# Top-1 and top-2 routing moved into the attention loop, tile by tile, in a hybrid decoder layer

## What is computed

```python
h2 = rms_norm(x2, ln2_g)
g_logits = h2 @ gw + gb                       # 4 expert groups
g_idx = argmax(g_logits); g_p = softmax(g_logits)[g_idx]
e_logits = (h2 @ ew + eb).reshape(T, 4, 8)[g_idx]
top_v, top_i = top_k(e_logits, 2)             # 2 of the group's 8 experts
gate = g_p * softmax(top_v); expert = g_idx * 8 + top_i
out = x2 + sum_r gate[r] * swiglu(h2, expert[r]);   final rms_norm
```

## Time and profile before

| | us |
|---|---|
| median of 3 runs | 1270.96 (1270.56 to 1271.1) |
| the profiled execution, its own time | 1266.62 |
| its span, first to last instruction | 1264.1 |
| TensorE busy in the span | 1139.6 |
| VectorE busy | 490.6 |
| ScalarE busy | 360.0 |
| GpSimd busy | 263.1 |

### The profile page before, as it was taken

The page is one execution under the profiler, slowest core; times in us unless marked ns, Lnnn a source line. Parts: engine busy times, 40 slices in busy tenths (PEclk is TensorE's granted clock), DMA queues, the critical chain, the costliest instruction groups (busy, mean ns, idle before and its releaser), DMA issues.

```text
span 1264.1 us, 16164 instructions
## 1 busy us (share of the span) xinstructions
PE 1139.6 (90%) x5013; PEld 548.1 (43%) x5014; DVE 490.6 (39%) x1018; ACT 360.0 (28%) x731; POOL 263.1 (21%) x226
## 2 busy tenths in 40 slices
PE   5999999998899999983699999989999999999930
PEld 4898444454356666643233333323333333333310
DVE  4360029942455666327323323322322332332217
ACT  3121100015465555310122232212322223222212
POOL 2010199920000000010211111121111111111113
PEclk9999999999799999995899999999999999999975
DMA  7317111012411111185590899999699998989036
GB/s 246 27 32 140 35 34 34 0 67 72 167 49 53 51 51 51 51 340 208 193 407 33 349 375 377 419 420 420 265 379 419 394 419 356 419 349 414 30 135 276
DMA packets 96315, 270.33 MB, mean 214 GB/s; under 512 B 42156, under 2 KB 59228, under 8 KB 71676
## 3 DMA queue, kind: packets, MB, share of 16 engines
q1 hardware_dynamic: 71060, 251.82, 52.0%
q0 software_dynamic: 8320, 16.80, 3.6%
q10 hardware_dynamic: 16872, 0.92, 0.9%
HBM read 253.25 MB, written 26.74 MB: 221 GB/s over the span
## 4 chain that ended last, share of the span: by engine, by line
PE 81%; DMA 7%; DVE 5%; ACT 2%; SPq 1%; issue 1%; ACTq 1%; POOLq 0%; POOL 0%; DVEq 0%
PE psum L1288 25%; PE psum L1021 13%; PE psum L1307 12%; PE psum L1203 9%; PE psum L1018 3%; PE psum L1161 3%; DMA W<-in_w_down 3%; PE psum L1181 2%; PE psum L1016 2%; PE psum L1276 2%; DMA W<-in_w_gate 2%; PE psum L1172 2%; PE psum L1295 2%; DMA W<-in_x 1%; PE psum L1226 1%
## 5 line engine op out<-in xcount | busy, mean ns | idle before, releaser
L1288 PE MATMUL psum<-W,RD 128*64 x800 | 366.8, 602 | 10.3 <-DVE RD L1775 10.3
L1289 PE MATMUL psum<-W,RD 128*64 128x512 f32 x800 | 366.8, 602 | 0.0
L1288 PEld LDWEIGHTS psum<-W,RD 128*64 128x64 f32 x800 | 106.2, 138 | 220.2 <-issue 214.3
L1307 PE MATMUL psum<-W,RD 128*64 x400 | 183.8, 602 | 3.2 <-ACT RD L944 2.4
L1308 PE MATMUL psum<-RD 128*64 128x512 f32 x400 | 183.8, 602 | 0.0
L1756 DVE TENSOR_TENSOR RD<-psum,RD 128x256 f32<-128x256 f32 x50 | 21.2, 424 | 414.2 <-ACT RD L940 414.2
L1021 PE MATMUL psum<-W 128*128 128x512 f32 x384 | 166.4, 593 | 0.6 <-ACT W L774 0.6
L699 POOL DMA_INDIRECT y_rows<-RD,tabi x49 | 51.9, 1059 | 472.8 <-ACT RD L951 453.5
L1203 PE MATMUL psum<-W,RD 128*128 128x512 f32 x256 | 120.0, 603 | 5.2 <-DVE W L1575 4.1
L1021 PEld LDWEIGHTS psum<-W 128*128 128x128 f32 x384 | 72.5, 190 | 89.7 <-issue 88.7
L1289 PEld LDWEIGHTS psum<-W,RD 128*64 128x64 f32 x800 | 106.2, 138 | 0.0
(11 more groups left out here) (315 smaller groups left out, 1290.7 us busy)
## 6 DMA issues: line engine op xcount, KB each, us to landing
W<-in_w_up SPq DMA_DIRECT2D x32, 2048.0 KB, 12.6
W<-in_w_gate SPq DMA_DIRECT2D x32, 2048.0 KB, 17.4
W<-in_w_down SPq DMA_DIRECT2D x32, 2048.0 KB, 19.2
W<-in_x SPq DMA_DIRECT2D x16, 512.0 KB, 5.0
W<-y_rows SPq DMA_DIRECT2D x16, 512.0 KB, 9.2
W<-in_w_in SPq DMA_DIRECT2D x5, 1024.0 KB, 12.6
W<-in_w_in SPq DMA_DIRECT2D x16, 256.0 KB, 4.3
x_rows<-W SPq DMA_DIRECT2D x8, 512.0 KB, 2.9
```

The costliest lines, as they stand in the source:

```text
L1288: pe.matmul(bank(2)[0:HALF].rearrange("p (g n) -> p g n", g=2), x, near, start=k == 0, stop=k == KD - 1)
L1289: ins = pe.matmul(bank(2)[HALF:P], x, upgate1[:, k].rearrange("p g n -> p (g n)"), start=k == 0, stop=k == KD - 1)
L1307: pe.matmul(out[0:HALF], a, W[:, bass.ds(base + (2 * KD * FF + D * k), 512)], start=k == 0, stop=k == FK - 1)
```

## The change

- The logits are made of x2 itself, not of h2: TensorE transposes x2 (`x2_turn`, half 0 at k = 4 i + 11, half 1 at k = 4 i + 13), multiplies at k = 4 i + 14, and VectorE multiplies with `rstd2` and adds the bias in one instruction. The loop has 44 iterations. h2 is still made and stored.
- VectorE picks the group (`pick_group`, k = 4 i + 14) and the experts (`pick_experts`, k = 4 i + 15) per tile. TensorE ranks tile i at k = 4 i + 18, ahead of the next tile's logits, with two bf16 matmuls (`rank`; `macc` is the sum of the tiles before). VectorE takes block and slot within the expert (`my_rank`, k = 4 i + 18) and writes `SI`, one-hot in the slot times the token's number.
- Behind the loop: the last tile's rank, the counts, the block numbers, 16 matmuls of 68 columns for the tokens, and the index table (`ids_ok`), on which the gathers start. The gates come after: VectorE turns `SI` into one-hot times gate (2048 elements), and TensorE does 16 more matmuls (`gate_ps`), ahead of the first turn of gathered rows. The table of blocks and experts has a block per partition and is turned into a row by 4 small matmuls. The first step's slot and counts are constants.
- `x2` has two buffers, not three; `xa` moves to where slot 0's gate goes, so that gate is loaded after the loop's last store; slot 2's down is loaded once the gates' matmuls have read `SI`.

```diff
-ITERS = 4 * (NT - 1) + 18
+ITERS = 4 * (NT - 1) + 16
@@ sync
-            load_gate(0)
             for i in range(NT):
 ...
+            load_gate(0)
             load_up(2)
             load_gate(2)
+            sp.wait_ge(gate_ps, 1)
             load_down(2)
@@ gpsimd
-            pool.wait_ge(idx_ok, 1)
+            pool.wait_ge(ids_ok, 1)
             for b in range(AHEAD):
                 gather(b)
+            pool.wait_ge(idx_ok, 1)
@@ tensor
+            def rank(i, out):
+                pe.wait_ge(mm_ok, i + 1)
+                ins = pe.matmul(out, tri[:, :], mbf[:, i, :], start=True, stop=i == 0)
+                if i:
+                    ins = pe.matmul(out, onesb[:, :], macc[:, i, :], start=False, stop=True)
+                return ins
 ...
-                    i = tile_at(k, 14 + b)
+                    i = tile_at(k, 11 + 2 * b)
                     if i is not None:
-                        h2_turn(i, b)
-                i = tile_at(k, 17)
+                        x2_turn(i, b)
+                i = tile_at(k, 14)
                 if i is not None:
+                    pe.wait_ge(h2T_ok, i + 1)
+                    if i:
+                        rank(i - 1, bank(5)[:, 64:96]).then_inc(rank_ps, 1)
                     logits(i)
 ...
+            rank(NT - 1, bank(0)[:, 0:32]).then_inc(rank_ps, 1)
+            pe.matmul(bank(1)[:, 0:32], onesb[:, :], macc[:, NT - 1, :], start=True, stop=False)
+            pe.matmul(bank(1)[:, 0:32], onesb[:, :], mbf[:, NT - 1, :], start=False, stop=True).then_inc(rank_ps, 1)
             for r in range(16):
                 if r % 8 == 0:
-                    pe.wait_ge(tab_ok, r // 8 + 1)
-                ins = pe.matmul(bank(2)[:, 0:2 * NBLK], slot1h[:, r, :], bval[:, r].rearrange("p n v -> p (n v)"),
-                                start=r == 0, stop=r == 15)
+                    pe.wait_ge(blk_ok, r // 8 + 1)
+                ins = pe.matmul(bank(2)[:, 0:NBLK], SI[:, r, :], blk1h[:, r, :], start=r == 0, stop=r == 15)
             ins.then_inc(tab_ps, 1)
 ...
+            pe.wait_ge(sg_ok, 1)
+            for r in range(16):
+                ins = pe.matmul(bank(3)[:, 0:NBLK], SI[:, r, :], blk1h[:, r, :], start=r == 0, stop=r == 15)
+            ins.then_inc(gate_ps, 1)
@@ vector
+            def pick_group(i):
+                dve.wait_ge(lg_ps, i + 1)
+                lg = logit[:, i, :]
+                dve.scalar_tensor_tensor(lg[:, 0:36], bank(5)[:, 0:36], rstd2[:, i:i + 1], rbias[:, :], ALU.mult, ALU.add).then_inc(lg_ok, 1)
+                dve.wait_ge(lg_ok, i + 1)
+                link(dve.max(mx8, lg[:, 32:40]))
+                dve.tensor_scalar(gdif[:, i, :], lg[:, 32:36], mx8[:, 0:1], None, ALU.subtract)
+                link(dve.max_index(gi8, mx8, lg[:, 32:40]))
+                link(dve.tensor_copy(gix[:, i:i + 1], gi8[:, 0:1]))
+                link(dve.tensor_scalar(goh, iotaf[:, 0:EGROUPS], gix[:, i:i + 1], None, ALU.is_equal))
+                link(dve.tensor_tensor(es4, ...))
+                link(dve.tensor_reduce(e8, es4.rearrange("p g n -> p n g"), AX.X, ALU.add))
+            def pick_experts(i):
+                link(dve.max(me8, e8))
+                dve.tensor_tensor(edif[:, i:i + 1], me8[:, 1:2], me8[:, 0:1], ALU.subtract)
+                link(dve.max_index(ei8, me8, e8))
+                dve.tensor_tensor(macc[:, i, :], macc[:, i - 1, :], mbf[:, i - 1, :], ALU.add)
+                link(dve.tensor_copy(idx2, ei8[:, 0:2]))
+                link(dve.scalar_tensor_tensor(idx2, idx2, float(EGROUPS), ...))
+                link(dve.tensor_tensor(MM[:, i], ..., ALU.is_equal))
+                dve.tensor_tensor(mbf[:, i, :], MM[:, i, 0, :], MM[:, i, 1, :], ALU.add).then_inc(mm_ok, 1)
+            def my_rank(i, src):
+                dve.wait_ge(rank_ps, i + 1)
+                dve.tensor_tensor(MP, MM[:, i], ..., ALU.mult).then_inc(rank_ok, 1)
+                dve.wait_ge(rank_ok, i + 1)
+                link(dve.tensor_reduce(rsel, MP, AX.X, ALU.add))
+                link(dve.tensor_scalar(lblk[:, i, :], rsel, ...))
+                link(dve.tensor_scalar(lblk[:, i, :], lblk[:, i, :], ROUND, ROUND, ALU.add, ALU.subtract))
+                link(dve.scalar_tensor_tensor(slot2, lblk[:, i, :], -float(HALF), rsel, ALU.mult, ALU.add))
+                for r in range(2):
+                    ins = dve.tensor_scalar(SI[:, 2 * i + r, :]..., slot2[:, r:r + 1], tokv[:, i, r:r + 1], ALU.is_equal, ALU.mult)
+                link(ins)
 ...
                 for b in range(2):
-                    i = tile_at(k, 14 + b)
+                    i = tile_at(k, 11 + 2 * b)
                     if i is not None:
-                        h2_turned(i, b)
+                        x2_turned(i, b)
+                i = tile_at(k, 14)
+                if i is not None:
+                    pick_group(i)
+                i = tile_at(k, 15)
+                if i is not None:
+                    pick_experts(i)
+                i = tile_at(k, 18)
+                if i is not None:
+                    my_rank(i, bank(5)[:, 64:96])
```

More of the change, by code:

```diff
@@ L254, in build, with late @@
+        d0 = 5120
+        def late(n):
+            nonlocal d0
+            d0 += n
+            assert d0 <= 5376
+            return RD[:, d0 - n:d0]
+        nb, bend, bs, ones, nn, below = late(32), late(32), late(32), late(32), late(6), late(32)
+        col = late(10)
+        stp = late(16)
+        gsum, den, gate = late(8), late(8), late(16).rearrange("p (t r) -> p t r", t=NT)
+        both = RD[:, 5700:5700 + 2 * NBLK].rearrange("p (n b) -> p n b", n=2)
         ident = sb("ident", [P, P])
@@ L425, in build @@
         ex_ye = sem("ex_ye")
-        x2_out = [sem(f"x2_out{i}") for i in range(3)]
+        x2_out = [sem(f"x2_out{i}") for i in range(2)]
         tail_y = sem("tail_y")
@@ L965, in step @@
                 actT_evac(b1)
+            step(0, 0)
             act.wait_ge(idx_ok, 1)
-            for b in range(4):
+            act.wait_ge(tabg_ok, 1)
+            for b in range(1, 4):
                 step(b // 2, b % 2)
@@ L1269, in _ @@
             ins.then_inc(tab_ps, 1)
+            pe.wait_ge(col_ok, 1)
+            for n_ in range(1 + SLOTS):
+                ins = pe.matmul(bank(7)[0:1, MAXBLK * n_:MAXBLK * (n_ + 1)], col[0:MAXBLK, n_:n_ + 1], ident[0:MAXBLK, 0:MAXBLK],
+                                start=True, stop=True)
+            ins.then_inc(col_ps, 1)
+            pe.wait_ge(sg_ok, 1)
+            for r in range(16):
+                ins = pe.matmul(bank(3)[:, 0:NBLK], SI[:, r, :], blk1h[:, r, :], start=r == 0, stop=r == 15)
@@ L1331, in step @@
                     down(bank(4 + (1 - q % 2)), prev, b, None if isinstance(freed, int) and freed <= 0 else freed)
+            xT(0, 16)
+            step(0, 0)
             pe.wait_ge(idx_ok, 1)
-            xT(0, 16)
-            for b in range(4):
+            for b in range(1, 4):
                 step(0, b)
@@ L1585, in _ @@
+            for k in range(ITERS):
+                if k == 6:
+                    dve.memset(logit, -3e38)
+                    dve.wait_ge(const_ok, 4)
+                    for r in range(2):
+                        ins = dve.tensor_scalar(tokv[:, :, r], tokf[:, :], 2.0, 2.0 * L * r - 4.0 * L, ALU.mult, ALU.add)
+                    link(ins)
                 for half in range(2):
@@ L1676, in _ @@
-            link(dve.reciprocal(gate[:, 0, :], den))
-            link(dve.tensor_tensor(gate[:, 1, :], gate[:, 0, :], eexp, ALU.mult))
-            dve.wait_ge(rank_ps, 1)
-            dve.tensor_copy(RK[:, :, :].rearrange("p t n -> p (t n)"), bank(0)[:, 0:256])
-            cnt, nb, bend, bs, ones = (ovt[:, 32 * q:32 * q + 32] for q in range(5))
+                    pick_group(i)
[3 more added lines that the diff above has]
+                i = tile_at(k, 18)
@@ L1712, in _ @@
-            nn = ovt[:, 160:166]
+            dve.tensor_tensor(bs, bend, nb, ALU.subtract)
+            my_rank(NT - 1, bank(0)[:, 0:32])
+            MMr = MM.rearrange("p t r n -> p (t r) n")
+            link(dve.tensor_tensor(QQ, MMr, bc(bs.unsqueeze(1), [P, 16, EXPERTS]), ALU.mult))
+            link(dve.tensor_reduce(stp, QQ, AX.X, ALU.add))
+            link(dve.tensor_tensor(stp, stp, lblk.rearrange("p t r -> p (t r)"), ALU.add))
+            for half in range(2):
+                c = slice(8 * half, 8 * half + 8)
+                dve.tensor_tensor(blk1h[:, c], bc(stp[:, c].unsqueeze(2), [P, 8, NBLK]), bc(iotaf[:, 0:NBLK].unsqueeze(1), [P, 8, NBLK]), ALU.is_equal).then_inc(blk_ok, 1)
@@ L1777, in step @@
                 dve.tensor_copy(dst[:, :, 4:8], src[:, :, 4:8]).then_inc(ex_cu, 1)
+            for s in range(2):
+                dve.wait_ge(x2_out[s], 16 * NT // 2)
             step(0, 0)
+            dve.wait_ge(gate_ps, 1)
+            dve.tensor_copy(tabg, bank(3)[:, 0:NBLK]).then_inc(tabg_ok, 1)
+            dve.wait_ge(idx_ok, 1)
             step(0, 1)
```

286 lines of the change are left out of this document (122 added, 164 removed).

## The result

The kernel takes 1274.51 us after the change (median of 20 runs, 1270.21 to 1280.32) and 1270.34 before it (20 runs on the same chips, 1266.0 to 1271.85). The ratio is 1.0043, 95% interval 1.003 to 1.0056: slower by 5.5 us by the ratio (the two medians lie 4.2 apart). I had forecast 3.7 us faster. The profiled execution of after took 1273.92, its span is 1272.2 us, that of before 1264.1.

The account below looks back on a forecast made before the run. Bound by TensorE's issue and waits in loop and experts, by a VectorE instruction chain in the routing between. Terms 3.5 + 5.5 - 6.5 - 4.9 - 1.3 = -3.7 took the median from 1270.96 to 1267.3 us; range 1262 to 1275.

Parts of the forecast that it names:

- chain (a): Loop, iterations 4 m + 2: pick_group and my_rank, 3.1 us on VectorE behind the logits, hidden by 1.8 us of slack.
- Stalls (b): Loop, iterations 16 to 31: pick_experts ahead of x2_half makes fill wait 0.41 to 1.04 us, four times: +2.9.
- Rank pairs +0.6: Loop, iterations 16 to 31: the rank's four pairs of bf16 matmuls on TensorE at 0.15 us each: +0.6.
- The second rival: The loop costs more: each chain takes 0.7 us more, +4 or more, so the gain is gone: 1271; chance 0.20.
- Tail +5.5: Iterations 32 to 43: pick_experts in full in three waits +4.1, logits replaced by turns -1.4, turns by rank and logits +2.8.
- Last x2 to last pick -6.5: Behind the loop: 18.5 us become 12.0, as one turn and the picks of seven tiles are gone.
- Last pick to experts -4.9: Routing behind the loop: 27.1 us become 22.2, each table's 16 passes taking 5.5, the gates' passes the last wait.
- The bound that I had written down, 7.3: Routing tables behind the loop: upper end of the 3.7 to 7.3 us given for 32 passes, where 5.5 was taken.
- Clock at the start -1.3: Experts' start: the first 2.7 us run at clock 1.00 instead of 0.50: -1.3, bounds 0 and -1.3.
- Loads, at nothing: Experts' first steps: slot 0's gate lands with 9 us of cover and slot 2's down meets idle DMA; costed at nothing.
- The first rival: The clock stays low in the tail, at both tables and at the experts' start: 7.5 us in all, 1274.8; chance 0.20.
- The third rival: VectorE's picks are cheaper, pick_experts 0.7 us, shrinking stalls, tail and the last tile's picks: 1260.6; chance 0.11.

Follow-up runs that it names:

- e9: The kernel before with the logits' 16 passes of tiles 2 and 3 (iterations 25 and 29) done twice: 1274.74 us, ratio 1.0037.
- e10: The kernel before with the logits' 16 passes of tile 6 (iteration 41, beside the last x2's square and variance) done twice: 1269.97 us, ratio 0.9992.
- e2: The changed kernel with the 16 gate matmuls moved behind the first block's up and gate matmuls: 1278.71 us, ratio to before 1.0094.
- e3: The changed kernel plus 124 bf16 matmuls, result never read, in TensorE's idle time behind the loop: 1268.42 us, ratio to before 0.9999.
- e4: The kernel before plus seven linked 8-element VectorE instructions on an unread buffer where pick_experts stands in the changed kernel: 1279.31 us, ratio 1.0096.
- e1: The changed kernel with pick_experts of tiles 0 to 6 one iteration later, behind x2_half and combine: 1264.93 us, ratio to before 0.9968.
- e5: The changed kernel with the later picks of e1 and 150 dummy matmuls placed at TensorE's waits behind the loop: 1257.29 us, ratio to before 0.9896.
- e6: e1 with the table built once, token and gate side by side in 136 columns, instead of twice: 1263.14 us, ratio to before 0.9937.

## Why the prediction was wrong

It had the sign wrong (slower, where faster was forecast), though 1274.5 lies at the upper end of its range. Three things in it failed: the clock was taken too high (at both tables, in the tail and at the experts' start), the cost of TensorE's work that moved ahead into the loop was never entered, and the slack of chain (a) was read 0.5 us too kindly. By its steps, profile against profile, from the 1262.9 forecast to the 1273.9 measured:

- **Stalls (b), four of them, +2.9: right.** The rows show 0.82, 0.60, 0.34 and 0.18, which is less than the 0.41 to 1.04 that I worked out, but the iterations are 3.0 longer in all.
- **Rank pairs +0.6: right.** 0.14 a pair.
- **Chain (a) "just hidden": wrong by 0.5.** Iterations 19, 23 and 27 took 0.28, 0.18 and 0.08 longer than before; the scores behind the first show it as a wait for ScalarE's exponentials:

```profile
419.57 1.56 PE L1183 MATMUL psum<-W 64*128 64x512 f32 x8 [0.20 <-ACT W L889]
```

In iteration 18 `pick_group` and `my_rank` lasted 3.5 us (412.44 to 415.97) where I had 3.1, and `stats` started 2.3 us late against a slack of 1.8. The second rival had this mechanism and priced it at 4.

- **Missing step, +2.1.** I costed where VectorE's work went and not where TensorE's did: the turns and logits of every tile moved three iterations ahead, one turn and one `logits` more into the full loop. I took the emptied place behind the last x2 as a gain in the term -6.5, which was right, and never booked the cost of the new place. e9 and e10 show it.
- **Tail +5.5: mechanism right, size 9.4.** +1.4 up to `fill` at k = 32 and -0.8 from there to k = 34 are near the forecast. At k = 36 came 0.75 more, a VectorE instruction held up by GpSimd (below). The rest, 2.9, is the clock: within the wait of 3.50 at k = 36 it went to 0.50, and iteration 36 to 37 took that much longer. The kept profiles agree on where: in the four with a wait of 2.82 to 3.50 us at k = 36 (after, e2, e3, e4) that `fill` took 5.25 to 6.61, and in the eight with 1.38 (before, e1, e5 to e10) it took 3.70. Long waits are not the only occasion: in e10, with the waits of before, the clock was at 0.50 twice elsewhere in the tail (533.4 to 536.8, and about 557.3 to 560.7).
- **Last x2 to last pick -6.5: right** (-6.3), as I had taken the logits at the low clock there.
- **Last pick to experts -4.9: the term that failed most** (-1.6). The chain is as forecast, the gates' passes the last wait, but I took 16 of each table's passes at the full clock "as in the row". In that row the clock rose in the midst of the table. It did so in each of the five profiles with one table of 136 columns and no dummies (before, e4, e6, e9, e10), but not within the first table of after, e1 or e2, nor within the second of after or e1: these ran at 0.22 a pass throughout, 7.1 each in after: +3.2. So the price was that of another kernel's table and no average; what keeps the rise away from the tables of 68 columns is open. The bound that I had written down, 7.3, was near the right value.
- **Clock at the start -1.3: wrong by 2.9** (+1.6). The gain didn't come: the experts of after start at 0.50 and stay there for 3.4 us, before's for 2.7. With the clock at 1.00 at the start the stage takes 654.2 us in e3 and 655.8 in e5, where it went to 0.50 for 3.4 us soon after, at 607.1. The other profiles (e2, with 664.4, left aside) lie between 654.3 and 658.3 with no tie to the start: before and e4 start at 0.50 and take 654.5 and 654.3. So 1 to 2 us of this term are no effect of the change that these profiles can show.
- **Loads, at nothing: right.** No DMA is among the releasers of the first expert steps' waits of TensorE.

0.5 + 2.1 + 0.75 + 2.9 + 3.2 + 2.9 is 12.35, less the 1.25 that the shorter low clock at iteration 8 gave after: 11.1. The stages divide the spans, and there 11.8 has to be found (8.1, and the 3.7 of the forecast); the 0.7 left is spread over the stages, 0.3 at most in one. That the sum meets the 11.0 between the executions is chance: after's execution lasts 1.7 longer than its span, where I had added 2.5.

The first rival ("the clock stays low", 0.20) is what happened: one fall in the tail, both tables at the low price, no gain at the start. Its 7.5 us are 9.0 in the rows (the 1 to 2 of the experts' stage that can't be tied to the clock among them), and with the missing step they outweigh the gain. I gave it too little because I argued that a burst of 32 passes brought the clock back: before and e6 show the rise inside such a burst, after shows two bursts without one. The third rival (cheap picks) is refuted: the last tile's `pick_experts` ran from 589.19 to 590.67, 1.48 us.

The Trainium skill, "TensorE: Matmul & The Clock Gate", Part 1, lets the moment of a clock change shift from run to run, as the prediction cites it. The runs fit that: executions of the kernel before have mean clocks from 0.951 to 0.958, and the averages of these two groups are 7.4 us apart. They don't show the moment itself.

## What to carry to other kernels

Work moved ahead into a full engine's stage costs nearly its full time there (1.8 us for 1.95 in e9), and a place that a chain left empty gives little back; book each moved piece twice, where it goes and where it leaves. In a merged stage the order on the helping engine matters more than its load: what frees the bank goes first, bookkeeping after (one iteration's delay of the picks turned +5.5 us into -4, by the ratios). And where a bottleneck engine has gaps, price its bursts at the low clock unless something keeps it at work, and take no average from a row in which the clock changed.

## What the runs showed of the hardware

**A VectorE instruction held up by GpSimd.** GpSimd's product of 512 columns (L695) and VectorE's small instructions around it, after:

```profile
550.35 1.05 POOL L695 TENSOR_TENSOR RD<-RD,hrstd 128x512 f32<-128x512 f32 x1
550.52 0.90 DVE L1649 TENSOR_TENSOR W<-W 128x32 bf16<-128x32 bf16 x1
...
551.35 0.16 DVE L1650 CAST W<-W 128x2 f32<-128x2 uint32 x1
...
552.11 0.68 DVE L1619 TENSOR_TENSOR W<-psum,W 128x512 f32<-128x512 f32 x1
```

The bf16 sum of two tiles in SBUF takes 0.90 instead of 0.17 and ends at 551.42, with GpSimd's instruction (551.40). It did so in e2 and e3 (0.90, 0.89). In e1, where the picks lie elsewhere, another instruction meets it:

```profile
548.12 1.05 POOL L695 TENSOR_TENSOR RD<-RD,hrstd 128x512 f32<-128x512 f32 x1
548.37 0.16 DVE L1643 MAX8 W<-W 128x8 f32<-128x8 f32 x1
548.56 0.62 DVE L1644 TENSOR_TENSOR edif<-W 128x1 f32<-128x1 f32 x1
```

548.56 + 0.62 is 549.18; GpSimd's ends at 549.17. So it isn't the type that counts, but that VectorE reads two operands from SBUF while GpSimd's product runs; the instructions with one operand beside it keep their 0.16. Beside GpSimd's small instruction of 4 elements (L692) nothing is held up: `combine`'s two-operand instruction (L1606) takes 0.22 there as everywhere. The other way round GpSimd is held up. Where VectorE's two-operand instruction of `combine` (L1608) is under way first, the product ends 0.91 us behind its end and shows up to 1.57 us (ends 519.87 and 520.78 in after) instead of 1.05. The Trainium skill, "SBUF — State Buffer", section "Who interferes with whom", says that such an instruction and GpSimd's reads exclude each other and that the second to issue waits in full. The traces agree, in both orders. In the changed kernel it stood on the path: 0.75 us.

**A pass of few columns has one price per clock.** 32 passes take 7.09 at 0.50 with 68 columns and 3.79 at 1.00; with 136 columns 4.15 at 1.00; the logits' 16 with 36 columns 3.61 and 1.95. So up to 136 columns hardly count (a tenth from 68 to 136 at 1.00), while the full clock nearly halves the time. At 0.50, 16 passes of 136 columns took 4.00 in e10, against 3.62 for 16 of 68 in after.

**The clock fell while TensorE was busy throughout,** in e9, within 4.1 us of 36-column passes, after 10 us in which TensorE had not been idle (455 to 465.5, at 1.00). The others that I looked at had a wait of TensorE just ahead: 3.50 us in after (until 552.85, the fall within it, at about 551.9), 2.29 in e5 (until 606.75, the fall at 607.1), 0.89 in e10 (until 532.34, the fall at 533.4). I had thought only of idle time.
